# Inverses of the 16x16 diagonal blocks on VectorE, behind on-chip transfers, in an RWKV-7 recurrence by chunks

## The reference

```python
def step(S, inp):
    r_t, w_t, k_t, v_t, kk_t, a_t = inp
    sa = jnp.einsum('bhvk,bhk->bhv', S, -kk_t)
    S = (S * w_t[:, :, None, :] + sa[..., None] * (kk_t * a_t)[:, :, None, :]
         + v_t[..., None] * k_t[:, :, None, :])
    return S, jnp.einsum('bhvk,bhk->bhv', S, r_t)
```

## Time and profile before

| | |
|---|---|
| median of 3 runs | 1786.02 us (1785.7 to 1789.13) |
| profiled execution, its own time | 1785.42 us |
| span of its profile | 1783.7 us |
| mean granted clock of TensorE, as a share of full speed | 0.948 |
| TensorE busy | 1628.9 us, 91% of the span, 17188 records |
| VectorE busy | 892.6 us, 50% |
| ScalarE busy | 459.2 us, 26% |

### The profile page before, as it was taken

One profiled execution on the slowest core, in us unless ns is written; L12 is line 12 of the kernel. 1 busy time (PEld: TensorE's weight loads), 2 busy tenths in 40 slices (PEclk: granted clock), 3 DMA queues, 4 the chain that ended last, 5 costly groups with the idle time before them and its releaser, 6 DMA issues.

```text
span 1783.7 us, 40832 instructions
## 1 busy us (share of the span) xinstructions
PE 1628.9 (91%) x17188; PEld 1513.3 (85%) x17188; DVE 892.6 (50%) x1196; ACT 459.2 (26%) x670; POOL 569.2 (32%) x353
## 2 busy tenths in 40 slices
PE   6899999998659999998897999977999999999995
PEld 6899999997229999997477989944999999999995
DVE  4489999432795656565652664042632112211247
ACT  4222222234441111111212234232233212211221
POOL 2555551136460000000144411201644534443541
PEclk9999999999659999999779999998999999999997
DMA  4212253224000000101413144245212222222222
GB/s 154 71 59 75 78 74 88 90 99 150 26 0 4 4 4 4 41 20 42 153 35 142 59 138 157 98 160 209 81 60 82 71 79 74 71 80 73 71 82 82
DMA packets 54749, 140.03 MB, mean 79 GB/s; under 512 B 22208, under 2 KB 24768, under 8 KB 52592
## 3 DMA queue, kind: packets, MB, share of 16 engines
q1 hardware_dynamic: 53360, 133.15, 23.5%
q0 software_dynamic: 1280, 5.24, 0.7%
HBM read 125.38 MB, written 12.99 MB: 78 GB/s over the span
## 4 chain that ended last, share of the span: by engine, by line
PE 55%; issue 19%; DVE 10%; POOL 10%; ACT 3%; DMA 1%; POOLq 0%; DVEq 0%; SPq 0%; ACTq 0%; PEldq 0%
PE ps L375 33%; PE ps L487 15%; POOL wlo L353 7%; POOL hdl L1695 2%; PE ps L1753 1%; DVE x L800 1%; PE ps L1874 1%; DMA kc<-in_kc 1%; DVE p_L L1396 1%; DVE ar L1453 1%; DVE acc L1300 1%; PE ps L1801 1%; PE ps L1773 1%; DVE ar L1416 1%; PE ps L1883 0%
## 5 line engine op out<-in xcount | busy, mean ns | idle before, releaser
L353 POOL TENSOR_TENSOR wlo<-raw,whi 128x1024 fp32r<-128x1024 f32 x150 | 382.7, 2551 | 555.1 <-ACT whi L342 554.7
L342 ACT ACTIVATE whi<-raw 128x1024 fp32r<-128x1024 f32 x158 | 166.7, 1055 | 282.7 <-PE ps L375 275.5
L375 PE MATMUL ps<-xnl,whi 128*128 128x320 f32 x672 | 154.5, 311 | 7.5 <-POOL xnl L444 6.1
L375 PE MATMUL ps<-fnl,whi 128*128 128x320 f32 x704 | 160.7, 309 | 0.0
L375 PE MATMUL ps<-fnh,wlo 128*128 128x320 f32 x704 | 160.5, 309 | 0.0
L375 PE MATMUL ps<-fnh,whi 128*128 128x320 f32 x704 | 160.3, 309 | 0.0
L375 PE MATMUL ps<-xnh,wlo 128*128 128x320 f32 x672 | 153.7, 310 | 0.0
L375 PE MATMUL ps<-xnh,whi 128*128 128x320 f32 x672 | 153.6, 310 | 0.0
L375 PEld LDWEIGHTS ps<-xnl,whi 128*128 128x128 f32 x672 | 113.1, 189 | 8.3 <-issue 6.4
L1300 DVE SCALAR_TENSOR_TENSOR acc<-up,vec,acc 128x512 f32<-128x512 f32 x240 | 118.3, 560 | 0.0
L375 PEld LDWEIGHTS ps<-fnl,whi 128*128 128x128 f32 x704 | 117.8, 188 | 0.3
(11 more groups left out here) (323 smaller groups left out, 3533.8 us busy)
## 6 DMA issues: line engine op xcount, KB each, us to landing
raw<-in_slots SPq DMA_DIRECT2D x174, 512.0 KB, 3.5
kc<-in_kc SPq DMA_DIRECT2D x4, 2048.0 KB, 8.7
vc<-in_vc SPq DMA_DIRECT2D x8, 1024.0 KB, 8.8
xin<-in_x SPq DMA_DIRECT2D x4, 640.0 KB, 8.0
tmp_g<-tmp POOLq DMA_DIRECT2D x8, 320.0 KB, 2.5
tmp_m<-pr POOLq DMA_DIRECT2D x8, 320.0 KB, 3.8
m1t<-tmp_m SPq DMA_DIRECT2D x1, 2560.0 KB, 11.7
t2t<-tmp_g SPq DMA_DIRECT2D x1, 2560.0 KB, 17.7
```

What stands on the lines that cost most here:

```text
L342: nc.scalar.activation(whi[s][:].rearrange("p a b -> p (a b)"), raw[s][:], ACT.Copy).then_inc(S["w_hi"], 1)
L353: on.tensor_tensor(wlo[s][:].rearrange("p a b -> p (a b)"), raw[s][:], whi[s][:].rearrange("p a b -> p (a b)").bitcast(F32), ALU.subtract) ...
L375: last = nc.tensor.matmul(cut(ps[s], h, n), a[:, k, :], b[:, k, h * w:(h + 1) * w], start=(k == 0 and q == 0), stop=(k == k_tiles - 1 and ...
```

## The change

TensorE keeps levels 4 and 5 of the prompt's chunks. Levels 0 to 3, which make the inverses of the 16 x 16 diagonal blocks, go to VectorE, for two chunks (m, a "pair") at once. There are 16 heads, four blocks per head and two chunks, so 128 blocks, one per partition.

1. `scores_b` of chunks 2m and 2m + 1 is issued on TensorE two chunks ahead. `scores_b_in` masks the scores, and sums the block diagonal into `nd` (64 rows of 16 per head).
2. `rec_blocks` on SyncE issues 16 on-chip transfers per pair (8 for each chunk) that lay the blocks out as one per partition (`blk`).
3. VectorE makes the inverses by blocks of 2, 4 and 8 (`inverse_start`, `inverse_level`, `inverse_end`), as elementwise products with broadcast operands and sums over the last axis. The three pieces stand between the odd chunk's other operations.
4. Another 16 transfers bring the inverses and their transposes back (`xd`). ScalarE places them on the diagonal of `x2` in four copies with a scale per partition (`inverse_in`), behind the outputs of the chunk.
5. `level_t(k, 0)` on TensorE waits for that (`x_made`). For the chunks of streams the placed blocks are the whole inverse.

`turn_v` uses another bank of PSUM (2 for 1), `scb` has four buffers (three new places), smk holds 3 masks for 8. The state loads stand behind `rec_blocks` in SyncE's order, and `stream_states` waits for all 16. Semaphores on which nothing waited are gone. The core of the diff:

```diff
+        nd = [stacked(f"nd{s}", 8, 16) for s in range(2)]
+        xd = [stacked(f"xd{s}", 8, 2, 16) for s in range(2)]
         assert o <= W_O + 63232, o
-        smk = at("smk", W_O + 63232, [P, LEVELS + 2, 64])
+        smk = at("smk", W_O + 63232, [P, 3, 64])
+        o = W_O + 64000
+        blk, inv, prod, half_prod = stacked("blk", 16, 16), stacked("inv", 16, 2, 16), stacked("prod", 512), stacked("half_prod", 64)
+        assert o <= W_O + 70016, o
...
+        def rec_blocks(sp, m):
+
+            for e in range(2):
+                sp.wait_ge(S["nd_ready"], nth(2 * m + e, 1))
+                if m and e == 0:
+                    sp.wait_ge(S["inv_step"], 2 + INV_STEPS * m)
+                for t in range(8):
+                    p0 = 64 * e + 8 * t
+                    sp.dma_start(blk[p0:p0 + 8, :, :], nd[e][:, t, :]).then_inc(S["block_in"], 16)
+            sp.wait_ge(S["inv_step"], 2 + INV_STEPS * (m + 1))
+            for e in range(2):
+                if m:
+                    sp.wait_ge(S["x_made"], 4 * (2 * m + e - 1))
+                for t in range(8):
+                    p0 = 64 * e + 8 * t
+                    sp.dma_start(xd[e][:, t, :, :].rearrange("p n c -> p (n c)"), inv[p0:p0 + 8, :, :, :].rearrange("p r n c -> p r (n c)"))\
+                        .then_inc(S["xd_in"], 16)
+
...
+            def scores_b(c):
+                for g in range(2):
+                    if c >= 2 and c % 2 == 0:
+                        w("bkt_in", nth(c - 2, g))
+                    elif c >= 2:
+                        w("x_new", lv(c - 3, 1, g))
                     for p in range(4):
                         t = 4 * g + p
-                        out = bank(g, 0)[:, P * p:P * p + P].rearrange("p (a c) -> p a c", a=2)
-                        last = heads(out, bt[:, t, rows_of(k)], ar[:, t, :, rows_of(k)])
+                        out = bank(g, 1 - c % 2)[:, P * p:P * p + P].rearrange("p (a c) -> p a c", a=2)
...
+            def level_t(k, l):
+                for g in range(2):
+                    if l:
+                        w("x_new", lv(k, 0, g))
+                    else:
+                        w("x_made", 4 * k + 4)
+                        if k % 2:
+                            w("nd_ready", nth(k + 2, g))
+                        elif k:
+                            w("x_new", lv(k - 1, 1, g))
+                        else:
+                            w("nd_ready", nth(1, g))
                     for p in range(4):
                         t = 4 * g + p
-                        last = heads(quarter(g, 0, p), scb[k % 2][:, t, 0:64], x2[k % 2][:, 0, t, :])
...
+                    if j < NCH:
+                        w("x_new", lv(j, 1, g))
+                    else:
+                        w("x_made", 4 * j + 4)
+                    if j == NCH:
+                        w("v_in", nth(j + 1, g))
...
-                pe.wait_ge(ss_in[i], 128)
+                pe.wait_ge(S["states_in"], 256)
                 for g in range(2):
                     if i:
                         w("y_in", nth(j - 1, g))
                     else:
-                        w("s_new", nth(j - 1, g))
+                        w("v_in", nth(j, g))
                     for p in range(4):
...
+            scores_b(0)
+            scores_b(1)
             for k in range(NCH + 1):
...
+                if k < NCH:
+                    level_t(k, 0)
                 turn_bk(k)
                 if k:
                     solve(j, 3)
-                level_t(k, 1)
+                if k < NCH:
+                    level_4(k)
                 if k:
                     new_state(j)
-                level_x(k, 1)
+                if k < NCH:
+                    level_t(k, 1)
+                if k < NCH and k % 2 == 0:
+                    scores_b(k + 2)
                 turn_v(k)
-                level_t(k, 2)
+                if k < NCH:
+                    level_5(k)
                 if k:
                     outputs(j, 3)
-                level_x(k, 2)
-                for L in range(3, levels(k)):
-                    level_t(k, L)
-                    level_x(k, L)
-            scores_b(NCH + 1)
+                if k < NCH and k % 2 == 0:
+                    scores_b(k + 3)
...
+            def inverse_in(c):
+
+                w("xd_in", 256 * (c // 2 + 1))
+                if c >= 2:
+                    w("u_psum", nth(c - 2, 1))
+                for q in range(4):
+                    nc.scalar.activation(x2[c % 2][:, :, :, 16 * q:16 * q + 16], xd[c % 2][:].rearrange("p t n c -> p n t c"), ACT.Copy,
+                                         scale=cst[:, CCOL["stream"] + q:CCOL["stream"] + q + 1]).then_inc(S["x_made"], 1)
...
+                inverse_in(k + 1)
...
+            def scores_b_in(c):
+                if c >= 2:
+                    w("block_in", 256 * (c // 2))
+                for g in range(2):
+                    w("scb_made", nth(c, g))
+                    tt(ndt[:, gs[g], :], four(bank(g, 1 - c % 2)[:, :])[:, :, 0:64], b4(wmask[:, 128:192]), ALU.mult).then_inc(S["nd_part"], 1)
+                    tt(scb[c % 4][:, gs[g], :], four(bank(g, 1 - c % 2)[:, :]), mask(c), ALU.mult)
+                    w("nd_part", nth(c, g))
+                    nc.vector.tensor_reduce(out=nd[c % 2][:, gs[g], :], in_=ndt[:, gs[g], :].rearrange("p t (q c) -> p t c q", q=4),
+                                            op=ALU.add, axis=AX.X).then_inc(S["nd_ready"], 1)
...
+            def product(m, n, size, left, right):
+
+                dve.wait_ge(S["inv_step"], 2 + INV_STEPS * m + n)
+                nb = 8 // size
+                out = prod[:, 0:nb * size ** 3].rearrange("p (b i c j) -> p b i c j", b=nb, i=size, c=size)
+                for b in range(nb):
+                    last = tt(out[:, b, :, :, :], left[:, b, :, :].rearrange("p i (c j) -> p i c j", c=1).to_broadcast([P, size, size, size]),
+                              right[:, b, :, :].rearrange("p j (i c) -> p i c j", i=1).to_broadcast([P, size, size, size]), ALU.mult)
+                last.then_inc(S["inv_step"], 1)
+                return out
+
+            def summed(m, n, out, terms):
+                dve.wait_ge(S["inv_step"], 2 + INV_STEPS * m + n)
+                nc.vector.tensor_reduce(out=out, in_=terms, op=ALU.add, axis=AX.X).then_inc(S["inv_step"], 1)
+
+            def inverse_level(m, size):
+
+                n = {2: 1, 4: 5, 8: 9}[size]
+                upper = diagonal_blocks(low, 32, 0, size)
+                corner = diagonal_blocks(low[:, size:, size:], 32, 0, size)
+                side = diagonal_blocks(low, 32, size, size)
+                given = diagonal_blocks(blk, 16, size, size)
+                part = half_prod[:, 0:8 * size].rearrange("p (b i c) -> p b i c", b=8 // size, i=size)
+                summed(m, n + 1, part, product(m, n, size, upper, given))
+                summed(m, n + 3, side, product(m, n + 2, size, part, corner))
+
+            def inverse_start(m):
+                w("block_in", 256 * (m + 1))
+                if m:
+                    w("xd_in", 256 * m)
+                dve.wait_ge(S["inv_step"], 2 + INV_STEPS * m)
+                nc.vector.tensor_copy(inv_flat[:, 17:512:66], blk_flat[:, 1:256:34]).then_inc(S["inv_step"], 1)
+                inverse_level(m, 2)
+
+            def inverse_end(m):
+                inverse_level(m, 8)
+                dve.wait_ge(S["inv_step"], 2 + INV_STEPS * m + 13)
+                nc.vector.tensor_copy(inv[:, 0:8, 0, :], low.rearrange("p a b -> p b a")[:, 0:8, :]).then_inc(S["inv_step"], 1)
+                nc.vector.tensor_copy(inv[:, 8:16, 0, :], low.rearrange("p a b -> p b a")[:, 8:16, :]).then_inc(S["inv_step"], 1)
+                dve.wait_ge(S["inv_step"], 2 + INV_STEPS * m + 15)
+                dve.sem_inc(S["inv_step"], 1)
...
+            scores_b_in(0)
+            scores_b_in(1)
+            inverse_start(0)
+            inverse_level(0, 4)
+            inverse_end(0)
...
+                ahead = k % 2 == 1 and k < NCH
+                scores_k_in(k)
+                if k < NCH:
+                    level_t(k, 0)
+                if ahead:
+                    inverse_start(m)
+                if k < NCH:
+                    level_4(k)
                 if k:
                     new_state(j)
-                level_x(k, 1)
-                for L in range(2, levels(k)):
-                    level_t(k, L)
-                    level_x(k, L)
+                if k < NCH:
+                    level_t(k, 1)
+                if ahead:
+                    inverse_level(m, 4)
+                if k < NCH and k % 2 == 0:
+                    scores_b_in(k + 2)
+                if k < NCH:
+                    level_5(k)
+                if ahead:
+                    inverse_end(m)
+                if k < NCH and k % 2 == 0:
+                    scores_b_in(k + 3)
...
+            for m in range(CHUNKS // 2):
+                rec_blocks(sp, m)
```

(62 more changed lines are left out.)

108 lines of the change are left out of this document (50 added, 58 removed).

## The result

The changed kernel takes 1774.74 us (median of 10 runs, 1767.02 to 1781.27) against 1785.86 us (10 runs, 1783.21 to 1789.13): a ratio of 0.9942, 95% interval 0.9925 to 0.9959. It is faster, as forecast, but by 11 us instead of 21.

A forecast was written before the change was run, and what follows sets the result against it. TensorE, busy for 91% of the span, was taken to bound the kernel. Fill +26.8, pairs -23.1, end (-8.6 - 3.7) and -12.0 sum to -20.6 us, giving 1765 us; range 1740 to 1801.

The forecast's parts named there:

- the fill: From the first scores until TensorE is in chunk 1, at 586.3 us instead of 559.48: 26.8 us lost.
- the pairs: Two prompt chunks together: 51.6 us against 59.3, so 7.7 us won, three times: 23.1.
- The end: From chunk 7, starting 3.7 us late, through the stream chunks: 8.6 us won by the first `stream_states`, then 12.0 more.
- 786.0, no later than TensorE: State loads, issued behind the last return, done at 786.0 us, with TensorE ready at 785.5.
- Together 22.2: 12.0 won: From the first `stream_states` to the second: 22.2 us instead of 34.2.
- The pitch: Time from one on-chip transfer's issue to the next on SyncE: 0.60 us, with 0.1 us of it worth 11.9 us.
- The placements: ScalarE's four copies of 256 columns, with their waits: 1.35 us a chunk.
- the inverse: VectorE's copy and products for sizes 2, 4 and 8: 6.3 us a pair.
- The half clock: TensorE at the lower clock behind every long stall: 2.5 us lost each time.
- (a): Slower: transfers drain more slowly than issued, perhaps over only 8 engines; 1795 us at a pitch of 0.85. Chance 0.29.
- (b): Only the issue costs: a pitch of 0.47 us, 15.5 us less, 1750 us. Chance 0.20.
- (c): Returns hidden and TensorE still the bound: pairs of 40.7 us plus old waits, 1721 us. Chance 0.03.

The follow-up runs named there:

- Experiment 2: Changed kernel with SyncE issuing the 16 state loads ahead of the last return instead of behind it: 1775.13 us, 0.9929 of the kernel before.
- experiment 5: Changed kernel with useless TensorE work at its end alone: 1776.04 us, 0.9931 of the kernel before; with the state loads also moved ahead: 1773.33 us, 0.9914.
- experiment 3: Changed kernel with each return's 16 transfers split, 8 on SyncE's queue and 8 on ScalarE's: 1756.24 us, 0.9839 of the kernel before.
- experiment 4: Changed kernel with TensorE computing useless scores while it waits for a return, to keep the clock up: 1775.35 us, 0.9945 of the kernel before.
- experiment 6: Changed kernel with each transfer of the second to fifth return carrying half its rows, so half the packets: one run, 1778.87 us.

## Where the prediction held and where it failed

**The mechanism** was right in the fill and in the pairs: TensorE's period shrank to the round trip of the blocks, with a wait of 12.6 to 13.4 us (forecast 11.7) ahead of chunks 2, 4 and 6, ended by a placement. Within a pair the steps agree to a tenth where nothing hiccuped: from the scores at 639.90 the blocks are there after 10.57 us (10.55) and the return begins after 21.41 (21.35); in part that is luck, as the terms below show.

**The end is the step that failed**: "786.0, no later than TensorE", and "Together 22.2: 12.0 won". The loads behind the last return landed at 793.3, TensorE had been ready since about 791.7, and it was 793.36 that the first `stream_states` began: 1.25 us earlier than before instead of 8.6. Of the 7.3 us by which the loads landed late, 5.5 came from the fill and the pairs, 1.6 from the last inverse and 0.9 from the issues of its return; the loads themselves took 15.1 us, near the 15.7 of the forecast. From there the stage took 49.5 us; before, it was 55.1, so 5.6 were won, not 12.0. Of the 13.8 us by which the stage missed its forecast, 6.4 lie in these two chunks (3.2 and 3.3), more than in any other part. The step that failed in them is the clock: the forecast had charged the lower clock to the long waits and nothing to the stream chunks, though the row of before showed 0.50 there already, ahead of the second `stream_states`. Experiment 2 shows it: the same instructions with the loads moved, so without the wait and at a granted clock of 1.00, run the first chunk in 22.25 us, as worked out. At the full clock the second takes 21.2 (experiment 5) or 19.7 us (experiment 3), where 20.8 had been kept from before.

**Mis-sized terms.** The other 7.4 us add up before the stream chunks: 2.5 in the fill, 3.0 in the pairs, 1.9 from the last pair to the states. The pitch was 0.645 instead of 0.60: 0.7 us for each train of 16. From the start of the last issue to the first placement it was 2.0 to 2.1 instead of 2.6. The placements took 0.35 us more each time. In the fill the inverse took 7.1 us instead of 6.3, for the products of 512 elements were priced by a row with other operands; in a pair the same 0.6 us was made up for by other steps, which were estimated too long. The half clock behind the wait of chunk 2 cost 1.7 to 2.0 us instead of 2.5 (an estimate of 1.3 to 2.7 over the three, see experiment 4), which went the other way.

**The rivals.** (a), the slow drain, is out: halving what one queue issues took 4.3 us off a return (experiment 3), and halving the packets 1 us (6). The engines' row says the same: busy for 0.13 of 12.14 us, 16 engines spent 25 us on 16 transfers, and if only 8 of them carried each, that is an estimate of 0.2 us for a transfer, a third of its issue. How many carry one is not shown. The counts fit 8: the trace has 2176 packets for a return, 136 for each transfer of 128 rows, and 68 for each of 64 rows in experiment 6, so 8 and 4 more than the rows, as many as there are partitions at the narrow side. Should these be one for each engine, experiment 6 halved the engines along with the packets and tells of the issue alone, not of the drain. (b), a price of 0.47, is out by the row of the issues. (c), pairs of TensorE's own length, did not come about with this order, and did as soon as the order gave the return a chunk's time: 1721 us was worked out for it, with pairs of 40.7 us; 1718.6 and 38.2 were measured, so the totals agree better than their parts. The half of the rule that bears on experiment 3 stands in the Trainium skill, DMA: Bandwidth & Descriptors, Issuing engines are not separate DMA queues: starting transfers from several engines saves only the sequencer's time to start them, and that is usually small beside the transfer. The trace agrees with the first half; not with the second, for here the issues are 10.4 of the 13.9 us of a return with its placement.

## What to carry to other kernels

A chain of many small transfers on one queue costs its issues, almost whatever they carry: count the issues between the last result and the first use, and either split them over the queues of engines that stand waiting anyway or start the chain so much earlier that it lies behind other work. What is queued behind such a chain (here the state loads) is late by all of it. And a forecast that takes work from TensorE has to ask of each stretch that it leaves bare what clock the same work will then run at, also where the waits are short.

## What was not expected of the hardware

- An on-chip transfer of 128 rows takes 0.604 us to issue, one of 64 rows 0.545: from these two, an estimate of 0.49 us for the transfer and 0.9 ns for a row. Single issues took up to 1.58 us (1.72 among the state loads), and each such one moves what waits behind it by up to 1 us.
- On VectorE a product of 512 elements whose two operands are both read with repeated elements took 1.03 us, 0.34 more than one of 512 read from PSUM and a mask; a reduction to 64 over a strided view of 256 took 0.58 us.
- A wait of 1.69 us ahead of the first `stream_states`, behind one of 10.85, went with a granted clock of 0.65 over the next 4.6 us (793.36 to 798) and with 3.2 us lost in that chunk: twice the wait itself.
